# Expert rows scaled and gated in one VectorE step and accumulated into the output, which is preloaded with residual and bias

## The reference, cut to what matters

```python
x = x + gate2(c) * moe_ffn(modulate(x, norm_ffn_w, shift, scale))
# moe_ffn: top 4 of 32 experts per token, p = softmax over the four logits
#   gu  = xb @ w_gate_up[e] + b_gate_up[e]                (1024 -> 2048)
#   act = (clip(up) + 1) * min(gate, 7) * sigmoid(1.702 * gate)
#   y   = act @ w_down[e] + b_down[e]                     (1024 -> 1024)
#   out[token] += p[token, e] * y
```

## Time and profile before

| | |
|---|---|
| median of 3 runs | 1874.53 us |
| profiled execution, its span | 1873.67 us, 1871.9 us |
| PE, DVE, ACT busy over the span | 95%, 77%, 59% |
| mean granted TensorE clock | 0.970 of full |
| DMA traffic | 500.40 MB, mean 267 GB/s |
| mixer / routing / experts / end | 0 to 642, to 688, to 1845, to 1872 us |

### The profile page before, as it was taken

One profiled execution on the slowest core, in us unless ns is written; L12 is line 12 of the kernel. 1 busy time (PEld: TensorE's weight loads), 2 busy tenths in 40 slices (PEclk: granted clock), 3 DMA queues, 4 the chain that ended last, 5 costly groups with the idle time before them and its releaser, 6 DMA issues.

```text
span 1871.9 us, 30540 instructions
## 1 busy us (share of the span) xinstructions
PE 1771.2 (95%) x10966; PEld 1374.2 (73%) x10966; DVE 1440.7 (77%) x1688; ACT 1103.2 (59%) x1165; POOL 369.4 (20%) x252
## 2 busy tenths in 40 slices
PE   5999896699999869999999999999999999999996
PEld 2444795465588758888888888888888888888884
DVE  3579435663234569999999999999999989989998
ACT  2142321554123227777777777777787777777773
POOL 4000610001000212122122122213223212312321
PEclk9899999899999959999999999999999999999997
DMA  9850000401322179999999999999999999999996
GB/s 335 299 206 1 3 5 3 163 1 46 135 91 91 37 268 348 371 370 367 368 366 370 366 368 368 363 366 366 365 365 365 367 368 366 369 365 364 369 361 231
DMA packets 251970, 500.40 MB, mean 267 GB/s; under 512 B 17243, under 2 KB 19352, under 8 KB 251717
## 3 DMA queue, kind: packets, MB, share of 16 engines
q1 hardware_dynamic: 239814, 481.41, 71.1%
q0 software_dynamic: 9648, 17.33, 3.7%
q10 hardware_dynamic: 2448, 0.78, 0.2%
HBM read 491.06 MB, written 26.23 MB: 276 GB/s over the span
## 4 chain that ended last, share of the span: by engine, by line
PE 62%; DVE 1%; issue 0%; ACT 0%; ACTq 0%; DVEq 0%
PE bank L2015 19%; PE bank L2013 19%; PE bank L2014 19%; PE bank L2010 2%; PE bank L2028 2%; PE bank L2000 1%; PE bank L2085 1%; DVE sb_mod L2299 0%; DVE sb_e_lo L2205 0%; ACT sb_e_hi L2091 0%; DVE sb_x L2301 0%; DVE sb_mod L2292 0%; DVE sb_x L2295 0%; ACT sb_y L2101 0%; ACTq L1952 0%
## 5 line engine op out<-in xcount | busy, mean ns | idle before, releaser
L2205 DVE TENSOR_TENSOR sb_e_lo<-sb_w_raw,sb_e_hi 128x2048 fp32r<-128x2048 f32 x388 | 875.7, 2284 | 1.8 <-ACT sb_e_hi L2091 1.7
L2091 ACT CAST sb_e_hi<-sb_w_raw 128x2048 fp32r<-128x2048 f32 x389 | 743.3, 1911 | 145.4 <-DMA sb_w_raw<-in_w_down_dram 65.9
L2013 PE MATMUL bank<-sb_e_hi,sb_x_hi 128*128 128x512 f32 x1032 | 409.6, 397 | 0.0
L2015 PE MATMUL bank<-sb_e_hi,sb_x_lo 128*128 128x512 f32 x1032 | 405.6, 393 | 0.0
L2014 PE MATMUL bank<-sb_e_lo,sb_x_hi 128*128 128x512 f32 x1032 | 404.7, 392 | 0.0
L2176 POOL TENSOR_TENSOR sb_tick<-sb_ones 128x1 f32<-128x1 f32 x64 | 158.5, 2477 | 849.7 <-DVE sb_row L2275 695.1
L2015 PEld LDWEIGHTS bank<-sb_e_hi,sb_x_lo 128*128 128x128 f32 x1032 | 194.4, 188 | 41.9
L2014 PEld LDWEIGHTS bank<-sb_e_lo,sb_x_hi 128*128 128x128 f32 x1032 | 194.7, 189 | 40.5
L2013 PEld LDWEIGHTS bank<-sb_e_hi,sb_x_hi 128*128 128x128 f32 x1032 | 195.0, 189 | 37.1
L2013 PE MATMUL bank<-sb_e_hi,sb_a_hi 128*128 128x512 f32 x512 | 206.3, 403 | 0.0
L2015 PE MATMUL bank<-sb_e_hi,sb_a_lo 128*128 128x512 f32 x512 | 200.9, 392 | 0.0
(11 more groups left out here) (447 smaller groups left out, 2385.9 us busy)
## 6 DMA issues: line engine op xcount, KB each, us to landing
sb_w_raw<-in_w_gate_up_dram SPq DMA_DIRECT2D x262, 1024.0 KB, 10.2
sb_w_raw<-in_w_down_dram SPq DMA_DIRECT2D x128, 1024.0 KB, 12.5
sb_ring<-in_w_in_dram SPq DMA_DIRECT2D x7, 2048.0 KB, 10.4
sb_x<-in_ada_w_dram SPq DMA_DIRECT2D x8, 1024.0 KB, 9.2
sb_mod<-in_ada_w_dram SPq DMA_DIRECT2D x8, 1024.0 KB, 11.4
sb_ring<-in_ada_w_dram SPq DMA_DIRECT2D x3, 2048.0 KB, 13.3
sb_x<-in_x_dram SPq DMA_DIRECT2D x2, 2048.0 KB, 12.8
sb_ring<-in_w_out_dram SPq DMA_DIRECT2D x2, 2048.0 KB, 7.9
```

The source lines that it names most:

```text
L2013: te.matmul(out, hi[:, k0 + k, :], w_hi, start=(first and k == 0 and what >= 2 * GU), stop=False)
L2015: mm = te.matmul(out, lo[:, k0 + k, :], w_hi, start=False, stop=(last and k == 3))
L2091: return sc.copy(g.e_hi[:, p % PARTS, :, :], raw(p))
L2205: return ve.tensor_tensor(g.e_lo[:, p % PARTS, :, :], raw(p), g.e_hi[:, p % PARTS, :, :].bitcast(F32), ALU.subtract).then_inc(split_done[p ...
```

## The change

The output tensor itself takes the place of `y_rows`. In the routing phase SP writes x to it, and a bias part, wT times (b_down * gate2), is added to it by four accumulating DMAs that POOL issues. In the loop, DVE does what ACT did: one step out of PSUM multiplies by the share and by gate2. The work at the end goes away. Cut to its core:

```diff
 def add_rows(g, po, sem):
-    po.indirect_dma_start(out=g.y_rows[:, :], ... bounds_check=SEQ + P - 1, ... compute_op=ALU.add)
+    po.indirect_dma_start(out=g.out[0], ... bounds_check=SEQ - 1, ... compute_op=ALU.add)
 # routing, SP
-            sp.wait_ge(*pool.at("x_slot"))
-            for t in range(NT + 1):
-                sp.dma_start(g.y_rows[P * t:P * t + P, :], g.x_slot[:, :]).then_inc(g.zeroed, 16)
+            for t in ts:
+                sp.dma_start(g.out[0, P * t:P * t + P, :], g.x[:, t, :]).then_inc(g.x_out, 16)
 # routing, POOL: after s3, before the memsets of job_of and x_slot
+            po.wait_ge(bias_in, 16 * 3)
+            po.tensor_tensor(g.b_gated[:, :], g.b_down[:, :], g.mod[0:N_EXP, 3, :], ALU.mult)
+            po.wait_ge(*pool.at("b_gated"))
 ...
-            po.wait_ge(g.zeroed, 16 * (NT + 1))
             gather_rows(g, po, g.row_of[:, 0:1])
+            po.wait_ge(g.x_out, 16 * NT)
+            for t in ts:
+                po.wait_ge(*act.at(f"b{t}1"))
+                po.dma_start(g.out[0, P * t:P * t + P, :], g.bias_rows[:, t, :], accum_op=ALU.add).then_inc(g.bias_out, 16)
 # routing, ACT: behind bias_hi
+            for t in ts:
+                for n in range(2):
+                    sc.wait_ge(*pe.at(f"b{t}{n}"))
+                    sc.copy(g.bias_rows[:, t, 512 * n:512 * n + 512], ps[2 + 2 * n][:, :]).then_inc(*act(f"b{t}{n}"))
 # routing, PE
+            def bias_part(t):
+                for n in range(2):
+                    if t:
+                        te.wait_ge(*act.at(f"b{t - 1}{n}"))
+                    te.matmul(ps[2 + 2 * n][:, :], g.wT[:, P * t:P * t + P], g.b_gated[:, 512 * n:512 * n + 512], ...)
     the four transposes for wT move from behind tok to between base and rank(NT - 1)
     after table and total:
+            te.wait_ge(*vec.at("wT"))
+            te.wait_ge(*vec.at("counts"))
+            te.wait_ge(*pool.at("b_gated"))
+            bias_part(0)
+            bias_part(1)
             te.wait_ge(*vec.at("in_tok"))          # the 16 tok matmuls follow, then the 16 of prob_of (bank 6 now)
+            for t in ts[2:]:
+                bias_part(t)
 # routing, DVE: chosen and weight (L1894, L1895) move to before counts; the copy wT (L1905)
 # moves to between b3 and js; in_prob (L1900) moves to before the wait for tok
 # experts, PE
-                te.wait_ge(*act.before("y0", turn))       # before w6; y1 before w7 likewise
+                te.wait_ge(*vec.before("y0", turn))
     the bias matmuls behind the loop (L2085) go
 # experts, ACT: both stores go; at the end a wait for the last loads and a one-column copy
 # experts, POOL
+            po.wait_ge(g.bias_out, 16 * NT)               # before the gather for the second job
     y1 is waited for from vec
 # experts, DVE
+            def store(n):
+                at = slice(512 * n, 512 * n + 512)
+                return ve.scalar_tensor_tensor(g.y[:, at], ps[4 + n][:, :], g.prob_now[:, 0:1], g.mod[:, 3, at], ALU.mult, ALU.mult)
+                ve.wait_ge(*pe.before("w11", turn))       # first in the turn, before lo(2)
+                store(1).then_inc(*vec("y1"))
                 lo(2)
 ...
                 lo(0)
+                ve.wait_ge(*pe.at("w10", turn))
+                store(0).then_inc(*vec("y0"))
                 lo(1)
     behind the loop: wait for the last w11, store(1); all of L2286 to L2301 goes
 # experts, SP: behind the loop only the wait for last_stored stays; read-back, output and their waits go
```

More of the change, by code:

```diff
@@ L1790, in _ @@
             te.matmul(ps[7][:, 0:N_EXP], block_sum[0:N_EXP, :], g.later[0:N_EXP, 0:N_EXP], start=True, stop=True).then_inc(*pe("base"))
+            te.wait_ge(*vec.at("weight"))
+            for t in ts:
+                mm = te.transpose(ps[3][0:N_EXP, P * t:P * t + P], weight[:, t, :], g.ident[:, :])
+            mm.then_inc(*pe("wT"))
             rank(NT - 1).then_inc(*pe("rank"))
@@ L1852, in _ @@
             then(ve.tensor_tensor(g.prob[:, :, :], ex, inv.unsqueeze(2).broadcast_to([P, NT, TOP_K]), ALU.mult), "prob")
+            then(ve.tensor_tensor(chosen, choice, wide(g.prob[:, :, :]), ALU.mult), "chosen")
+            ve.tensor_reduce(weight, chosen.rearrange("p t k e -> p t e k"), AX_X, ALU.add).then_inc(*vec("weight"))
             ve.wait_ge(*pe.at("count"))
@@ L1893, in _ @@
             ve.tensor_scalar(up, up, 1.0, None, ALU.add).then_inc(*vec("bias_up"))
-            then(ve.tensor_tensor(chosen, choice, wide(g.prob[:, :, :]), ALU.mult), "chosen")
-            ve.tensor_reduce(weight, chosen.rearrange("p t k e -> p t e k"), AX_X, ALU.add).then_inc(*vec("weight"))
+            share = g.prob[:, :, :].rearrange("p t k -> p (t k)")
+            ve.tensor_tensor(in_job, in_job, share.unsqueeze(2).broadcast_to([P, units, JOBS]), ALU.mult).then_inc(*vec("in_prob"))
             ve.wait_ge(*pe.at("tok"))
@@ L1943, in phase_experts @@
         first_vec = g.steps(ctx, "first_vec", ["y", "share", "bp", "xl0", "xl1", "uc0"])
[L1944 to L1948, removed]
+        last_vec = g.steps(ctx, "last_vec", ["y1"])
         block = ctx.enter_context(nc.Block())
@@ L2066, in _ @@
                 features(1, 6).then_inc(*pe("xt1"))
-                te.wait_ge(*act.at("y1", turn))
+                te.wait_ge(*vec.at("y1", turn))
                 down(7, turn)
@@ L2080, in _ @@
             te.wait_ge(*vec.before("ac0", jobs))
[L2081 to L2086, removed]
         @block.scalar
@@ L2164, in _ @@
                 hi(1)
-                sc.wait_ge(*pe.at("w10", turn))
-                sc.wait_ge(*vec.at("goal", turn))
-                store(0).then_inc(*act("y0"))
                 hi(2)
-            sc.wait_ge(*pe.before("w11", jobs))
-            store(1).then_inc(*last_act("y1"))
+            sc.wait_ge(*loaded(3, jobs))
+            sc.copy(g.unused[:, 3:4], g.ones[:, 0:1]).then_inc(last_load, 1)
         @block.gpsimd
@@ L2282, in _ @@
                 lo(0)
+                ve.wait_ge(*pe.at("w10", turn))
+                store(0).then_inc(*vec("y0"))
                 lo(1)
             ve.memset(g.unused[:, 1:2], 0.0).then_inc(last_goal, 1)
[L2286 to L2292, removed]
-                mm.then_inc(*last_vec(f"gb{t}"))
-                ve.wait_ge(*last_vec.at(f"gb{t}"))
-                ve.tensor_tensor(g.x[:, t, :], g.x[:, t, :], g.mod[:, t % 3, :], ALU.add).then_inc(*last_vec(f"xb{t}"))
-            for t in ts:
-                ve.wait_ge(back_in[t], 16)
-                ve.wait_ge(*last_vec.at(f"out{t - 3}" if t >= 3 else "xb3"))
-                ve.tensor_tensor(g.mod[:, t % 3, :], back(t), g.mod[:, 3, :], ALU.mult).then_inc(*last_vec(f"gate{t}"))
-                ve.wait_ge(*last_vec.at(f"gate{t}"))
-                ve.tensor_tensor(g.x[:, t, :], g.x[:, t, :], g.mod[:, t % 3, :], ALU.add).then_inc(*last_vec(f"out{t}"))
+            ve.wait_ge(*pe.before("w11", jobs))
+            store(1).then_inc(*last_vec("y1"))
 def decoder_layer(nc, a, out):
```

64 lines of the change are left out of this document (23 added, 41 removed).

## The result

The changed kernel is slower by a quarter of a per cent: 1878.14 us median of 14 runs (1874.48 to 1882.08) against 1873.09 us for 14 runs of the kernel before, ratio 1.0024 [1.0013, 1.0035], or +4.5 us (the medians themselves lie 5.05 apart). The profiled execution took 1878.28 us with a span of 1876.2 us, so 4.3 us more span than before. The forecast was 2.5 us less, at 1872 us, and 1878.14 lies outside its own range of 1868 to 1877.

What follows compares the result with a forecast made beforehand. PE was taken to bound the early turns, transfers just behind in late ones, with serial routing and end. The sum, -17.9 end, 0 loop, +15.4 routing, was -2.5 us: 1872 us, own range 1868 to 1877 (8 in 10: 1862 to 1884).

Steps and rivals of the forecast that it cites:

- Step 1: Routing: DVE's cast of 16 columns waits for POOL's multiply of b_down by gate2, +1.2 us.
- Steps 2 and 3: Routing: chosen and weight on DVE cost 0; the copy of wT before js delays the rank step, +1.1 us.
- Step 4: Routing: bias_part(1), ahead of tok on PE, waits for ACT's copy behind bias_hi; tok starts 7.9 us later.
- Step 5: Routing: prob_of follows tok at once on PE, which is free at 694.7.
- Step 6: End of routing: last bias parts, ACT's copy and POOL's DMA issue put the meeting at 703.8, not 688.4: +15.4 us.
- The loop: Expert loop: two stores a turn move from ACT to DVE, which has time free; cost 0.
- The tail: After the last expert matmul: the last add's landing becomes the end, 1854.0 instead of 1871.9, saving 17.9 us.
- A: Routing: the low clock ends early, near 686, halving 15 us of matmuls; -7.5 us, time 1864; chance 0.17.
- B: Loop, lo(2) before w2: DVE becomes the bound, 0.4 us a turn, +12.8, time 1885; chance 0.13.
- C: Routing: engines need not meet, so only the tok delay (+9.1) counts; 1866 or less; chance 0.06.

Runs made afterwards that it cites:

- b2: The changed kernel with bias_part(1) in two other banks, so that it waits for no ACT copy; 1875.99 us, ratio 0.9995.
- b1: The changed kernel with the four bias DMAs issued at the start of POOL's expert part instead of in routing; 1876.21 us, ratio 1.0000.
- c1: The changed kernel with POOL waiting by semaphore for its last DMAs before the end of each of the two blocks; 1879.84 us, ratio 1.0035.
- a2: The kernel before with one 0.5 MB accumulating DMA from POOL to spare rows of y_rows after prob_of; 1884.07 us, ratio 1.0051.
- t3: The changed kernel without the add behind the loop, leaving out the last job's rows; 1874.57 us, ratio 1.0004.
- f1: The changed kernel with fp32r bias matmuls in PE's gap before tok, four banks, POOL's multiply halved, bias DMAs before the gather; 1861.93 us, 0.9939 against the kernel before.
- a1: The kernel before with only the loop's part of the change, both stores on DVE; 1880.12 us, ratio 1.0020.

## Why the prediction was wrong

- *Step 1 (+1.2):* right. The cast took 1.94 instead of 0.75 and ended with POOL's multiply at 659.9. The rule of the Trainium skill (SBUF — State Buffer, Who interferes with whom) that was weighed there holds: the cast lasts until the other engine's instruction is over.
- *Steps 2 and 3 (0, +1.1):* right. The copy behind `js` started at 669.38, where 668.2 + 1.2 was forecast. Rank came 2.26 later, steps 1 and 3 together.
- *Step 4 (tok +7.9):* right in its mechanism, and +9.2 measured, because step 1's 1.2 was added only in step 5. b2 shows that the wait for the copy behind bias_hi is 6.7 us of it.
- *Step 5 (PE free at 694.7):* 695.4 measured, tok and prob_of being 0.5 us longer together than priced.
- *Step 6 (the meeting at 703.8):* this is the step that failed. POOL's last issue ended at 704.3, close to the forecast, in part by luck: PE and ACT were 1.0 us later than priced, and POOL took 1.1 us from ACT's last copy where 1.6 was taken. But "a bias DMA still in flight delays only the gather for job 1" is wrong. The block does not end until POOL's queue has drained, and that is 0.2 us after its last DMA has landed: 709.3, 5.0 us behind the last issue, for which the sum had nothing. b1, with the DMAs elsewhere, has a routing phase 6.2 us shorter, c1 turns the drain into an explicit wait of the same length, and a2 shows it without the rest of the change. I had read for the meeting which instruction ended last on each engine; the view that was missing is the queues' drains at the block's end, which in the trace of before had POOL level with DVE, without any slack.
- *The loop (0):* right. Both stores fit (0.74 and 0.75, 0.68 forecast), and most of the 1.6 us between the profiles (1.45) appears between two profiles of the same kernel.
- *The tail (-17.9):* -15.0. The store 1.0 later and the landing 8.5 us behind the last matmul (1864.74 to 1867.24 + 6.0) came as forecast (8.5). "This landing is the end" failed: POOL's drain lasted 2.8 us more. Before, a drain of 9.03 us from 1846.7 on lay hidden below the end's arithmetic.
- *The rivals:* A did not happen, the clock was 0.50 from 660 to 710. B did not, the turns are 35.65. C (no meeting) did not, and the reverse of it did: the meeting costs more than the last issue.

So 5.6 us in routing and 2.9 in the tail were missed, 8.5 in all, less the 1.6 by which this profile's loop was shorter: -2.5 became +4.3 (4.4 from the rounded parts). Of the 5.6, 5.0 is the wait behind the last issue and the rest the later issue. Both misses lie in one thing overlooked, the drain of POOL's queue, but only that of routing is shown to be the wait for a landing; why the one at the end goes on for 2.8 us more stays open.

## What to carry to other kernels

Where engines meet, ask of each queue when its last transfer has landed, not when its last instruction ended: in these runs a DMA issued by GpSimd late in a block moved the meeting to its landing (the drain lasted 5.9 us from the issue on here, 8.4 in a2), so issue it early, or behind the meeting. Work added to a chain should first be looked for a place in idle stretches of all the engines that it needs; here the bias part cost 21 us in one place and type and 3 in another. Shortening a chain that ends in a transfer can bring that transfer under other traffic and lose part of the gain.

## What was unexpected of the hardware

- POOL's queue takes 5.37 and 5.45 us to drain at the end of the kernel even where its last transfer has landed (t3, c1), but 0.47 at the end of routing (c1). With an add in flight it is 9.0 (before, after), 2.8 beyond the landing. What it does in the 5.4 us stays open. That an indirect DMA stood ahead of it is not the reason: at the end of routing the drain ended 0.1 to 0.3 us after the landing also where the last DMA was an indirect gather (before, b1, f1). The loop ahead of it and the end of the kernel are left, and no run tells these apart.
- With PE idle for 1.83 us (1845.34 to 1847.17) instead of 0.85 (1845.44 to 1846.29) ahead of the last eight bias matmuls (sixteen passes), the granted clock fell near 1848 instead of near 1850.5, and they took 3.0 us more (a1).
- An accumulating DMA of 0.5 MB, issued last, held the block for 5.9 us where the weight loads were over (after) and for 8.4 to 8.6 with loads in flight (a2, b2).
- At one DMA share (1.02 to 1.05) the accumulating DMAs move 206 GB/s, plain writes 405 and loads 390 (after).
